# A buffer in front of the weight halves grows by 64 bytes

## The chip, the cores and the metric

The kernel runs on one core of one Trainium2 chip, in one launch. The metric is the device time of the whole program in microseconds (us); lower is better. Most executions of one kernel agree within 0.3%.

## The reference

The input is a sequence of 256 tokens of width 1024, in fp32. It passes through two layers of one kind and one of another, and all matrix products are fp32:

```python
for l in range(2):
    mod = silu(c) @ ada_w[l] + ada_b[l]                     # nine vectors of 1024
    x = x + 0.5 * g1 * swiglu(modulate(rms_norm(x)), w_gate, w_up, w_down)   # d_ff = 2816
    h = modulate(rms_norm(x)); z = h @ w_in[l]
    x = x + g2 * (concat(pool(z), mla_attention(z)) @ w_out[l])
    x = x + 0.5 * g3 * swiglu(modulate(rms_norm(x)), ...)
x = rms_norm(x)
# then one hybrid layer: S5 state-space mixer beside attention, then again
x = x + rmsnorm(swiglu(rmsnorm(x), w_gate, w_up, w_down))   # d_ff = 2816
```

There are five feed-forward networks (FFNs) with `swiglu(h) = (silu(h @ w_gate) * (h @ w_up)) @ w_down`. The S5 mixer needs the powers of a rotation, cos and sin of n times an angle for n up to 255.

## The kernel before

**Products in three passes.** Every weight and every activation of the large products is split into a high part of type fp32r and the rest. Line 539 (`passes`) then makes each product from three matmuls: high by high (L541), high by low (L542), low by high (L543). TensorE reads two operands from SBUF for each: the weights, which a weight load (LDWEIGHTS, "PEld" in the profile) puts into the array, and the moving operand. The profile lists the moving operand first: `gu_bank<-hT_hi,gu_hi` moves hT_hi past the weights gu_hi.

**An FFN.** Its hidden width is cut into 22 blocks of 128. For each block, `gate_up` runs 2 x 8 x 3 = 48 matmuls of 256 columns with weights from gu_hi and gu_lo, and `down` runs 4 x 3 = 12 matmuls of 512 columns with weights from act_hi and act_lo, moving dn_hi and dn_lo. Beside it SyncE loads raw_gu (1 MB) and raw_dn (0.5 MB) for later blocks, ScalarE copies them into gu_hi and dn_hi (L1037, L1043), and VectorE subtracts to get gu_lo and dn_lo (L1374, L1389). ScalarE and VectorE also turn the block's result into act_hi and act_lo (L1049, L1394, L1398, L1400). All of it is double buffered.

**The modulation.** VectorE sums 72 chunks of the matrix ada, 1 MB each, into acc_m and acc_g (L1315, L1325), in spare time beside the FFNs. GpSimd issues most of the loads into `stage`; the first eight come from SyncE into `pro`, `ring` and `stage` at the start of the program.

**The order of the work** is written by hand for each engine, with semaphores between them; no scheduler decides it.

**The buffers.** SBUF addresses follow from the order in which `program` makes the buffers: each starts behind the one before it, at a multiple of 32 bytes, and buffers of one stage share the room of another's. The address of a buffer is the same in all 128 partitions. All that lies behind `wpow` in this order is concerned by the change. Start addresses in bytes (per partition), with the place of each within 128 bytes:

| buffer, or the part that an instruction reads | start | within 128 |
|---|---|---|
| x, xn, hT, hT_hi, hT_lo, raw_gu, raw_dn, dn_hi, dn_lo, ring, gate_b | 16,512 to 118,912 | 0 |
| unit matrix and `fold` in cst | 123,240; 123,752 | 104 |
| ones | 132,576 | 96 |
| cz, its 32-column pieces 128 bytes apart | 133,696 | 64 |
| wpow, 320 bytes | 138,304 | 64 |
| stage, and in its room later ecos | 138,624 | 0 |
| acc_m (later esin), acc_g (later row_b) | 155,008; 175,488 | 0 |
| pro; gu_hi; z; u2 | 183,680 | 0 |
| gu_lo; qn | 200,064 | 0 |
| act_hi, act_lo | 220,544; 222,592 | 0 |
| pieces 0 and 2 of upad, behind their 16 columns of padding | 212,416; 214,592 | 64 |
| the four sums of pooling, behind their padding | from 216,768 | 64 |

All the rows with 0 lie 128 bytes past a multiple of 256.

`wpow` itself (rows 0 and 1: cos and sin of the present power; 2 to 4: scratch) is used while the table of rotations is built:

```python
w_c, w_s = (wpow[:, r, ss_].unsqueeze(2).to_broadcast(wide) for r in (0, 1))   # L1621
step.did(dve.tensor_tensor(wpow[:, 2, :], wpow[:, 0, :], wpow[:, 0, :], ALU.mult))   # L1631
step.then(dve.tensor_tensor(wpow[:, 4, :], wpow[:, 0, :], wpow[:, 1, :], ALU.mult))  # L1633
```

Of the kernel before, what the change touches and what calls it, by code (L numbers as in the profile page):

```python
# [24 lines left out]
P = 128  # L25
# [24 lines left out]
ST = 16  # L50
# [59 lines left out]
def program(nc, x_in, positions, consts, cols, gate_rows, rows, ada, ffn_gu, ffn_dn, mix_w, mix2_w, out):  # L110
    ctx = ExitStack()
    with ctx:
# [6 lines left out]
        def sb(stack, name, shape, dt=F32):  # L119
            return stack.enter_context(nc.sbuf_tensor(name, shape, dt))  # L120
# [30 lines left out]
        cim = sb(ctx, "cim", [P, ST])  # L151
        cz = sb(ctx, "cz", [P, 2, ST, 2, 16])
        sp = sb(ctx, "sp", [P, 8, ST])
        wpow = sb(ctx, "wpow", [P, 5, ST])
        ident = cst[:, C_ID:C_ID + P]
        fold = cst[:, C_FOLD:C_FOLD + P]
        mask = cst[:, C_MASK:C_MASK + 384]
# [1790 lines left out]
```

## Time and profile before

| | |
|---|---|
| median of 3 runs | 1384.41 us (1383.36 to 1385.72) |
| the profiled execution, its own time | 1385.61 us |
| its span, first to last instruction | 1383.8 us |
| mean granted clock of TensorE | 0.967 of full speed |
| TensorE busy | 95% of the span, 8744 matmuls |
| VectorE, ScalarE, GpSimd busy | 76%, 44%, 10% |
| moved by DMA | 296 MB |

The span is one execution seen by the hardware profiler; 1.8 us of that execution's time lie outside it. "Busy" is the union of an engine's instructions. Matmuls overlap in a pipeline, so the mean duration of one (286 ns) is longer than the distance from one start to the next, and what a matmul costs is read from the starts in the timeline.

### The profile page before, as it was taken

Reading aid. Unit: us, or ns where it says so; the run is one execution under the profiler, and the core shown is the slowest. Engines: PE = TensorE matmul, PEld = TensorE weight load, DVE = VectorE, ACT = ScalarE, POOL = GpSimd, SP = SyncE. Lnnn points to the kernel's source line nnn. Section 1 sums busy time; section 2 is a strip of 40 time slices with the busy share of each in tenths; the row PEclk is TensorE's granted clock in tenths of the full one; section 3 lists DMA queues with packets and bytes.
Section 4 is the critical chain, followed back from the end, with each engine's and each line's share of the span. In section 5 each row is a group of like instructions: output and inputs, shape, how many; then the busy total and the mean of one; then the engine's idle time right before and its main releaser. Section 6 shows DMA issues by size and latency. Waiting matters only on the chain.

```text
span 1383.8 us, 21395 instructions
## 1 busy us (share of the span) xinstructions
PE 1308.9 (95%) x8744; PEld 1198.2 (87%) x8744; DVE 1053.2 (76%) x1380; ACT 607.8 (44%) x868; POOL 136.0 (10%) x156
## 2 busy tenths in 40 slices
PE   1999999999999999999999999999978889899998
PEld 1899998989999998999999889999976667899997
DVE  7788887777879548888877868999469996755554
ACT  4533334576333336433345663333362235633333
POOL 0000100000005000100000000000007770000000
PEclk8899999998999999999999989999989989899999
DMA  9699896442886644988974417444442203354541
GB/s 373 254 357 349 339 361 260 144 146 92 305 311 248 261 166 141 361 329 334 352 287 156 160 67 276 182 183 182 184 151 77 76 28 124 144 190 189 189 185 46
DMA packets 55774, 296.12 MB, mean 214 GB/s; under 512 B 6560, under 2 KB 6816, under 8 KB 32416
## 3 DMA queue, kind: packets, MB, share of 16 engines
q1 hardware_dynamic: 46496, 228.21, 45.5%
q0 software_dynamic: 9216, 67.11, 12.2%
q8 instruction: 36, 0.59, 0.2%
q14 instruction: 26, 0.21, 0.0%
HBM read 294.25 MB, written 1.05 MB: 213 GB/s over the span
## 4 chain that ended last, share of the span: by engine, by line
PE 83%; DVE 11%; ACT 3%; issue 2%; DMA 1%; SPq 0%; DVEq 0%; ACTq 0%
PE gu_bank L541 17%; PE gu_bank L543 17%; PE gu_bank L542 17%; PE y_bank L541 8%; PE y_bank L542 8%; PE y_bank L543 8%; DVE ysc L1766 2%; DVE dn_lo L1369 2%; PE t_bank L541 1%; PE t_bank L543 1%; PE t_bank L542 1%; PE t_bank L527 1%; DVE acc_m L1315 1%; DVE vin L1761 1%; DMA pro<-ada 1%
## 5 line engine op out<-in xcount | busy, mean ns | idle before, releaser
L541 PE MATMUL gu_bank<-hT_hi,gu_hi 128*128 128x256 f32 x1760 | 504.2, 286 | 6.5 <-DVE hT_lo L1356 6.5
L542 PE MATMUL gu_bank<-hT_lo,gu_hi 128*128 128x256 f32 x1760 | 502.0, 285 | 0.0
L543 PE MATMUL gu_bank<-hT_hi,gu_lo 128*128 128x256 f32 x1760 | 501.9, 285 | 0.0
L541 PEld LDWEIGHTS gu_bank<-hT_hi,gu_hi 128*128 128x128 f32 x1760 | 341.7, 194 | 12.8 <-issue 9.0
L542 PEld LDWEIGHTS gu_bank<-hT_lo,gu_hi 128*128 128x128 f32 x1760 | 341.9, 194 | 4.7 <-issue 1.0
L543 PEld LDWEIGHTS gu_bank<-hT_hi,gu_lo 128*128 128x128 f32 x1760 | 341.6, 194 | 0.0
L1374 DVE TENSOR_TENSOR gu_lo<-raw_gu,gu_hi 128x2048 fp32r<-128x2048 f32 x105 | 241.1, 2296 | 47.6 <-ACT gu_hi L1037 47.4
L1049 ACT ACTIVATE sg<-gu_bank 128x256 f32<-128x256 f32 x110 | 42.2, 384 | 482.6 <-PE gu_bank L543 482.6
L1037 ACT ACTIVATE gu_hi<-raw_gu 128x2048 fp32r<-128x2048 f32 x105 | 200.6, 1911 | 9.2 <-DMA raw_gu<-ffn_gu 9.2
L541 PE MATMUL y_bank<-dn_hi,act_hi 128*128 128x512 f32 x440 | 172.8, 393 | 0.0
L542 PE MATMUL y_bank<-dn_lo,act_hi 128*128 128x512 f32 x440 | 172.5, 392 | 0.0
L543 PE MATMUL y_bank<-dn_hi,act_lo 128*128 128x512 f32 x440 | 171.2, 389 | 0.0
L1394 DVE TENSOR_TENSOR prod<-sg,gu_bank 128x256 f32<-128x256 f32 x110 | 46.1, 419 | 146.3 <-ACT sg L1049 145.6
L1043 ACT ACTIVATE dn_hi<-raw_dn 128x1024 fp32r<-128x1024 f32 x110 | 116.5, 1059 | 68.2 <-PE y_bank L543 68.2
L1389 DVE TENSOR_TENSOR dn_lo<-raw_dn,dn_hi 128x1024 fp32r<-128x1024 f32 x110 | 134.8, 1226 | 11.0 <-ACT dn_hi L1043 11.0
L468 POOL DMA_DIRECT2D stage<-ada x64 | 36.6, 572 | 793.9 <-DVE acc_g L1325 526.9
L1369 DVE TENSOR_TENSOR dn_lo<-ring,dn_hi 128x1024 fp32r<-128x1024 f32 x70 | 86.5, 1244 | 29.4 <-ACT dn_hi L1015 28.8
L543 PEld LDWEIGHTS y_bank<-dn_hi,act_lo 128*128 128x128 f32 x440 | 82.6, 188 | 18.0
L1015 ACT ACTIVATE dn_hi<-ring 128x1024 fp32r<-128x1024 f32 x70 | 73.5, 1055 | 52.2 <-PE gu_bank L543 23.9
L541 PEld LDWEIGHTS y_bank<-dn_hi,act_hi 128*128 128x128 f32 x440 | 83.0, 189 | 15.4 <-issue 1.0
L1315 DVE SCALAR_TENSOR_TENSOR acc_m<-stage,c_act,acc_m 128x2048 f32<-128x2048 f32 x37 | 87.4, 2363 | 9.7 <-DMA stage<-ada 9.2
L542 PEld LDWEIGHTS y_bank<-dn_lo,act_hi 128*128 128x128 f32 x440 | 83.0, 189 | 13.1
(337 smaller groups left out, 1801.0 us busy)
## 6 DMA issues: line engine op xcount, KB each, us to landing
raw_gu<-ffn_gu SPq DMA_DIRECT2D x110, 1024.0 KB, 5.9
stage<-ada POOLq DMA_DIRECT2D x64, 1024.0 KB, 7.5
raw_dn<-ffn_dn SPq DMA_DIRECT2D x110, 512.0 KB, 3.7
ring<-mix_w SPq DMA_DIRECT2D x72, 512.0 KB, 3.6
pro<-ada SPq DMA_DIRECT2D x5, 1024.0 KB, 12.1
gate_b<-gate_rows SPq DMA_DIRECT2D x6, 512.0 KB, 3.8
stage<-ada SPq DMA_DIRECT2D x2, 1024.0 KB, 20.4
x<-x_in SPq DMA_DIRECT2D x1, 1024.0 KB, 6.1
```

The lines of the kernel that those rows point to most:

```text
L541: pe.matmul(to, a[0], b[0], start=start, stop=False)
L542: pe.matmul(to, a[0], b[1], start=False, stop=False)
L543: return pe.matmul(to, a[1], b[0], start=False, stop=stop)
L1015: act.activation(dn_hi[:, (m + 2) % SLOTS, :], ring[:, n % RING, :], ACT.Copy).then_inc(w_hi_done, 1)
L1037: act.activation(gu_hi[:, b, :, :, :].rearrange("p h c n -> p (h c n)"), raw_gu[:, b, :], ACT.Copy).then_inc(gu_hi_done, 1)
L1043: act.activation(dn_hi[:, b, :], raw_dn[:, b, :], ACT.Copy).then_inc(dn_hi_done, 1)
L1049: act.activation(sg[:, b, :], gu_bank[b][:, 0:S], ACT.Silu).then_inc(silu_done, 1)
L1315: acc.did(dve.scalar_tensor_tensor(to, src, c_act[:, at:at + 1], to, ALU.mult, ALU.add))
L1369: dve.tensor_tensor(dn_lo[:, (m + 2) % SLOTS, :], ring[:, n % RING, :], dn_hi[:, (m + 2) % SLOTS, :].bitcast(F32), ALU.subtract).then_inc( ...
L1374: dve.tensor_tensor(gu_lo[:, b, :, :, :].rearrange("p h c n -> p (h c n)"), raw_gu[:, b, :], gu_hi[:, b, :, :, :].rearrange("p h c n -> p ...
L1389: dve.tensor_tensor(dn_lo[:, b, :], raw_dn[:, b, :], dn_hi[:, b, :].bitcast(F32), ALU.subtract).then_inc(dn_lo_done, 1)
L1394: dve.tensor_tensor(prod[:, b, :], sg[:, b, :], gu_bank[b][:, S:2 * S], ALU.mult).then_inc(prod_done, 1)
```

## The change

`wpow` gets a sixth row of 16 numbers. No instruction reads or writes it. The buffers that are made behind `wpow` start 64 bytes further on. The instructions of every engine, their number, order and shapes stay as they are; only start addresses differ.

```diff
-        wpow = sb(ctx, "wpow", [P, 5, ST])
+        wpow = sb(ctx, "wpow", [P, 6, ST])
```

So stage, acc_m and acc_g (and ecos, esin, row_b), ma and mb, pro, gu_hi, gu_lo, act_hi, act_lo, and all of the mixers' working buffers move from 0 to 64 within 128 bytes, or from 64 to 0. x, xn, hT and its halves, the raw weights, dn_hi, dn_lo, ring, gate_b, cst, ones and cz stay where they are.

## Rows read from the trace of the kernel before

**Rows 1.** The page: busy time, share of the span, instructions; the granted clock in slices.
```profile
PE 1308.9 (95%) x8744; PEld 1198.2 (87%) x8744; DVE 1053.2 (76%) x1380; ACT 607.8 (44%) x868; POOL 136.0 (10%) x156
...
PEclk8899999998999999999999989999989989899999
```

**Rows 2.** The page: the chain of work that ended last, by engine, share of the span.
```profile
PE 83%; DVE 11%; ACT 3%; issue 2%; DMA 1%; SPq 0%; DVEq 0%; ACTq 0%
```

**Rows 3.** The page's groups: line, engine, op, names, shapes, count | busy us, mean ns.
```profile
L541 PE MATMUL gu_bank<-hT_hi,gu_hi 128*128 128x256 f32 x1760 | 504.2, 286 | 6.5 <-DVE hT_lo L1356 6.5
...
L541 PE MATMUL y_bank<-dn_hi,act_hi 128*128 128x512 f32 x440 | 172.8, 393 | 0.0
```

**Rows 4.** Timeline of TensorE inside an FFN: start us, duration us, instruction.
```profile
603.27 0.40 PE L541 MATMUL y_bank<-dn_hi,act_hi 128*128 128x512 f32 x1
603.50 0.40 PE L542 MATMUL y_bank<-dn_lo,act_hi 128*128 128x512 f32 x1
...
606.01 0.28 PE L541 MATMUL gu_bank<-hT_hi,gu_hi 128*128 128x256 f32 x1
606.13 0.28 PE L542 MATMUL gu_bank<-hT_lo,gu_hi 128*128 128x256 f32 x1
```

**Rows 5.** Timeline of TensorE in a mixer, weights from dn_hi.
```profile
250.17 0.28 PE L541 MATMUL t_bank<-hT_hi,dn_hi 128*128 128x256 f32 x1
250.29 0.28 PE L542 MATMUL t_bank<-hT_lo,dn_hi 128*128 128x256 f32 x1
```

**Rows 6.** Timeline of ScalarE and VectorE over one block of that FFN.
```profile
603.47 0.38 ACT L1049 ACTIVATE sg<-gu_bank 128x256 f32<-128x256 f32 x1 [4.63 <-PE gu_bank L543]
...
611.97 0.39 ACT L1049 ACTIVATE sg<-gu_bank 128x256 f32<-128x256 f32 x1 [4.63 <-PE gu_bank L543]
...
606.44 2.29 DVE L1374 TENSOR_TENSOR gu_lo<-raw_gu,gu_hi 128x2048 fp32r<-128x2048 f32 x1
608.64 1.22 DVE L1389 TENSOR_TENSOR dn_lo<-raw_dn,dn_hi 128x1024 fp32r<-128x1024 f32 x1
```

**Rows 7.** Groups of weight loads, whole trace; the weights are the last name.
```profile
L541 PEld LDWEIGHTS gu_bank<-hT_hi,gu_hi 128*128 128x128 f32 x1760 | 341.7, 194 | 12.8 <-issue 9.0
...
L641 PEld LDWEIGHTS y_bank<-sq,ones 128*128 128x128 f32 x20 | 3.5, 191 | 0.3
...
L703 PEld LDWEIGHTS t_bank<-kn,qn 128*128 128x128 f32 x16 | 2.7, 191 | 0.2
...
L671 PEld LDWEIGHTS y_bank<-rot,cst 128*128 128x128 f32 x4 | 0.6, 190 | 0.0
```

**Rows 8.** Groups of plain fp32 matmuls, whole trace; the moving operand is named first.
```profile
L641 PE MATMUL y_bank<-sq,ones 128*128 128x256 f32 x20 | 5.0, 379 | 0.0
...
L703 PE MATMUL gu_bank<-kn,qn 128*128 128x256 f32 x8 | 2.4, 380 | 0.0
...
L684 PE MATMUL gu_bank<-sumA,ring 128*128 128x256 f32 x4 | 1.2, 379 | 0.0
```

**Rows 9.** Groups of ScalarE: copies and squares out of PSUM, 256 columns.
```profile
L1091 ACT ACTIVATE sq<-gu_bank 128x256 f32<-128x256 f32 x6 | 2.2, 365 | 0.0
...
L1073 ACT ACTIVATE upad<-gu_bank 128x256 f32<-128x256 f32 x4 | 1.5, 365 | 0.0
```

**Rows 10.** Groups of VectorE with two inputs in SBUF.
```profile
L1374 DVE TENSOR_TENSOR gu_lo<-raw_gu,gu_hi 128x2048 fp32r<-128x2048 f32 x105 | 241.1, 2296 | 47.6 <-ACT gu_hi L1037 47.4
L1389 DVE TENSOR_TENSOR dn_lo<-raw_dn,dn_hi 128x1024 fp32r<-128x1024 f32 x110 | 134.8, 1226 | 11.0 <-ACT dn_hi L1043 11.0
L1315 DVE SCALAR_TENSOR_TENSOR acc_m<-stage,c_act,acc_m 128x2048 f32<-128x2048 f32 x37 | 87.4, 2363 | 9.7 <-DMA stage<-ada 9.2
...
L1494 DVE TENSOR_TENSOR sumA<-upad 128x1084 f32<-128x1084 f32 x2 | 2.6, 1288 | 3.5 <-ACT upad L1073 3.5
```

**Rows 11.** The page: DMA issues, KB each, median us from issue to landing.
```profile
raw_gu<-ffn_gu SPq DMA_DIRECT2D x110, 1024.0 KB, 5.9
stage<-ada POOLq DMA_DIRECT2D x64, 1024.0 KB, 7.5
```

**Rows 12.** The chain that ended last, in order of time: its first long piece.
```profile
3.59 12.06 DMA pro<-ada
```

**Rows 13.** Timeline of TensorE at the start of a later FFN, and windows with the granted clock (last but two).
```profile
332.24 0.41 PE L543 MATMUL gu_bank<-hT_hi,gu_lo 128*128 128x256 f32 x1
332.45 0.41 PE L541 MATMUL gu_bank<-hT_hi,gu_hi 128*128 128x256 f32 x1
...
332.00:334.00 2.00, 2.00 (x11) 2.00 (x11) 2.00 (x4) 1.88 (x4) 0.00 (x0) 0.50 0.57 238
336.00:338.00 2.00, 2.00 (x18) 2.00 (x18) 1.98 (x1) 1.98 (x2) 0.00 (x0) 0.97 0.00 0
```

## The prediction

> **What bounds the kernel now.** The change moves addresses and nothing else, so the question is which instructions touch a moved address, and whether they are the ones that set the time. I read the busy shares first, then the chain that ended last, then the spacing of matmuls in the timeline. TensorE is busy for 95% of the span [rows 1] and holds 83% of the chain [rows 2]. Most of that is the FFN: three groups of 1760 matmuls on gu_bank and three of 440 on y_bank, of which one each is shown [rows 3]. Inside an FFN the matmuls start 0.12 us apart at 256 columns; the twelve of 512 columns take 606.01 - 603.27 = 2.74 us, 0.228 us each [rows 4]. One block is 48 x 0.120 + 2.74 = 8.50 us, and from one block's sg to the next it is 611.97 - 603.47 = 8.50 us [rows 6]. So nothing but matmuls stands in the block: it is bound by TensorE's own pace, which is the same in every block. ScalarE and VectorE have room: the gu_lo that is made from 606.44 to 608.73 is wanted when the next down (12 matmuls, from about 611.8) is over, near 614.5, some 5.8 us later, and the dn_lo that ends at 609.86 is wanted near 611.8, 1.9 us later [rows 6].
>
> **What the 64 bytes touch on TensorE.** These are the weights of all 5280 gate/up matmuls (gu_hi, gu_lo) and of all 1320 down matmuls (act_hi, act_lo): 6600 of the 8744. The moving operands of the FFN (hT_hi, hT_lo, dn_hi, dn_lo) stay. Before, weights and moving operands all start at 0 within 128 bytes; afterwards the weights start at 64. The spacing has a part that does not scale with columns: 256 columns more cost 0.228 - 0.120 = 0.108 us, so some 12 ns of each matmul are fixed [rows 4]. This is the part a weight load can reach, and the whole effect hangs on it. **Cost taken: 0.** The reasons are rows in which an operand already starts elsewhere. Weight loads of 128 columns take 191 ns from qn (0 within 128), 191 ns from ones (96) and 190 ns from fold in cst (104) [rows 7]; gu_hi's 194 ns is the longest of these four, though it starts at 0, so 64 bytes are not what makes a load long. Matmuls of 256 plain fp32 columns take 380 ns when both operands start at 0 (kn, qn), 379 ns when the weights start at 96 (sq, ones), and 379 ns when the moving operand starts at 64, as the pooling's sums do (sumA, ring) [rows 8]. That last row is the very shift of this change, on the other operand. In the mixers, with weights from dn_hi, the matmuls also start 0.12 us apart [rows 5]; within 512 bytes dn_hi starts at 128 and gu_hi at 384, so at least a shift by 256 bytes does nothing. What no row shows is an fp32r weight load that starts at 64 within 128. Its bounds come from the fixed 12 ns. Upwards: if a load of 512 bytes went in pieces of 128, it would meet five pieces in place of four, 12 / 4 = 3 ns more for each, and 6600 x 3 = 20 us. Downwards: if weights and moving operand hindered each other because they start alike, the 12 ns could go, 6600 x 12 = 79 us less. The nearest rows (rows 7 and 8) differ by 1 ns at most, in both directions and without order, so I take 0 and treat the two ends as rivals.
>
> **ScalarE.** It writes gu_hi, sg and the mixers' buffers at moved places. Two of the four pieces of upad start at 64 and two at 0 within 128; the mean of their writes is 365 ns, as for sq, which starts at 0 [rows 9]. Cost 0. Were each copy 10% longer (0.19 us on 1.9), it would still lie in the 5.8 us before gu_lo is wanted.
>
> **VectorE.** Its subtractions read one or two moved buffers. 1024 columns take 1226 ns and 2048 take 2296 ns, 1.045 ns a column. The pooling's first sum reads upad twice, one element (4 bytes) apart, over 1084 columns: the line gives 1226 + 60 x 1.045 = 1289 ns, measured 1288 ns [rows 10]. Operands that are out of step by 4 bytes cost nothing, so 64 bytes should not. Cost 0, with 1.9 us of cover in a block if that is wrong; outside the FFNs VectorE's 11% of the chain [rows 2], 152 us, has no such cover, and even 1 ns in 400 there would be 0.4 us. The instructions on wpow itself keep their lengths and places within a partition.
>
> **DMA.** Of the loads, those of ada move (64 from GpSimd's queue, seven of the first eight from SyncE's), and a few into row_b and wg; the raw weights stay. The trace has no row that isolates a load by its start within 128 or 256 bytes, so I bound it. Where a load stands in the chain it is once, 12.06 us for the first chunks [rows 12]; the waits of acc_m on stage come to 9.2 us in all [rows 10], inside the cover above. Two kinds of 1 MB load land in 5.9 and 7.5 us [rows 11], 27% apart for reasons of queue and traffic. If the move cost as much, the start would be 12.06 x 0.27 = 3.3 us longer; if it gave as much, 3.3 us shorter. Both kinds start at the same place within 256 bytes, so their difference is no sign of an effect of place, and I take 0, keeping ±3.3 us for the bounds.
>
> **The sum.** TensorE 0, ScalarE 0, VectorE 0, DMA 0. The profiled execution took 1385.61 us, 1383.8 of them in the span; the same is expected of the kernel after it. Against the median of the runs, 1.2 us lower, the forecast is 1384.4 us.
>
> **Rivals.**
> (a) *Slower: the weight load pays for its start.* Each of the 6600 loads becomes longer in the part that is not hidden behind the matmul before it. For it: this is the one thing that no row shows, and TensorE has no slack, so all of it would count. Against it: rows 7 and 8. It decides from 2.8 us / 6600 = 0.42 ns a load. At 1 ns it gives 1384.4 + 6.6 = 1391 us, at 3 ns 1404 us.
> (b) *Faster: the two reads of TensorE get out of each other's way.* The fixed 12 ns shrink by some or all: 1378 us at 1 ns, 1305 us at 12. The other engines would allow it, since a block would be 60 x 12 ns = 0.7 us shorter and the tightest cover is 1.9 us. For it: the fixed part is a delay beyond the columns, since at the lower of the two clocks (granted 0.50, 1.2 GHz) the spacing is 0.21 us, hardly more than the 0.108 us of 256 columns at full clock doubled [rows 13]. Against it: where the starts differ, in fp32, nothing is gained [rows 8], and the fixed part is the same with weights from dn_hi [rows 5].
> (c) *The start of the program moves.* DMA into pro and stage is slower or faster by up to 3.3 us: 1381.1 to 1387.7 us. Only the first 35 us would show it. Most of this lies within what three runs differ by.
> A change that does nothing at all is the forecast itself: I would not be able to tell it from one that costs a tenth of a nanosecond a load.
>
> **How the numbers follow.** No change: 0.84. Rival (a): 0.07. Rival (b): 0.04. Rival (c) in its outer part, beyond 0.2%: 0.05, of which 0.03 slower and 0.02 faster. A measurement of this kernel can tell about 0.2%, 2.8 us, from no change: the three runs differ by 2.4 us. That gives faster 0.06, same 0.84, slower 0.10. The range takes in no change with its spread (1384.4 ± 2.8) and a little of (c) on the upper side: 1381.5 to 1387.8 us, and leaves out some 15 in 100.
>
> **What the profile after would show.** If right: gate/up matmuls 0.12 us apart, down matmuls 0.23, a block of 8.50 us; gu_bank groups at 283 to 286 ns, gate/up weight loads at 194 ns; gu_lo at 2.29 us, gu_hi at 1.91; TensorE's granted clock at 0.967 within a few thousandths, with its dips at the same places, between the FFNs and at the start [rows 1]. If (a) or (b): a spacing other than 0.120 in gate/up while the mixers' matmuls on dn_hi keep theirs. If (c): everything behind the first matmul shifted by a constant, with the first chunks landing at another time. The forecast is wrong above all if the fp32r load reads memory in another way than the plain fp32 one, since my rows for other starts are plain fp32; and it would be wrong without any of this if the clock of TensorE were granted differently, since matmuls at the lower clock are 0.21 us apart in place of 0.12 [rows 13].

## The result

| | before | changed |
|---|---|---|
| median | 1384.4 us | 1359.7 us (1359.1 to 1361.9, four runs) |
| ratio | | 0.983, 95% interval 0.981 to 0.984 |
| span of the profiled execution | 1383.8 us | 1357.3 us |
| TensorE busy | 1308.9 us | 1282.4 us |

The kernel is 24.7 us faster, 1.8%, where no change was forecast. The page of the changed kernel gives busy times, the granted clock and the costliest groups:

```profile
PE 1282.4 (94%) x8744; PEld 1167.1 (86%) x8744; DVE 1050.6 (77%) x1380; ACT 608.8 (45%) x868; POOL 136.3 (10%) x156
...
PEclk8899999999999998999999989999989989999999
...
L541 PE MATMUL gu_bank<-hT_hi,gu_hi 128*128 128x256 f32 x1760 | 494.6, 281 | 8.3 <-DVE hT_lo L1356 8.0
...
L541 PEld LDWEIGHTS gu_bank<-hT_hi,gu_hi 128*128 128x128 f32 x1760 | 334.2, 190 | 15.7 <-issue 9.6
...
L1374 DVE TENSOR_TENSOR gu_lo<-raw_gu,gu_hi 128x2048 fp32r<-128x2048 f32 x105 | 241.0, 2295 | 40.5 <-ACT gu_hi L1037 40.5
...
L541 PE MATMUL y_bank<-dn_hi,act_hi 128*128 128x512 f32 x440 | 173.9, 395 | 0.0
```

TensorE's busy time fell by 26.5 us, just as much as the span; VectorE's subtraction takes 2295 ns as before (2296, [rows 10]) and the granted clock dips in the same stages as before, some dips shorter and some longer [rows 1]. Where TensorE gained is seen in its timeline (start, duration, instruction): the twelve down matmuls from 600.23 to 603.02, then gate/up.

```profile
600.23 0.39 PE L541 MATMUL y_bank<-dn_hi,act_hi 128*128 128x512 f32 x1
600.45 0.40 PE L542 MATMUL y_bank<-dn_lo,act_hi 128*128 128x512 f32 x1
...
603.02 0.28 PE L541 MATMUL gu_bank<-hT_hi,gu_hi 128*128 128x256 f32 x1
603.14 0.28 PE L542 MATMUL gu_bank<-hT_lo,gu_hi 128*128 128x256 f32 x1
...
603.48 0.28 PE L542 MATMUL gu_bank<-hT_lo,gu_hi 128*128 128x256 f32 x1
...
603.93 0.28 PE L543 MATMUL gu_bank<-hT_hi,gu_lo 128*128 128x256 f32 x1
```

From 603.02 to 603.93 are eight steps, 0.114 us each, against 0.120 before [rows 4]. The twelve down matmuls take 2.79 us against 2.74: they became slower. Over all starts in the two traces the mean step from a gate/up matmul to the next instruction fell from 122.0 to 116.3 ns (the slow clock's steps are in both means), 5280 x 5.7 = 30.1 us; from a down matmul it rose from 229.1 to 233.0 ns, 1320 x 3.9 = 5.1 us. The difference, 25.0 us, is 94% of the 26.5. The clock has little part in it: 88 gate/up steps ran at the lower clock before and 67 after, 21 x 0.1 = 2 us, and TensorE's waits at the starts of the second and fifth FFN, some 2 us longer, take that back. The other 1.5 us lie in the steps of the other matmuls (1.7 us less) and ahead of the first one (0.3 us more).

Of these 1.7 us, 0.4 have the cause that the experiments will show. 192 matmuls of the mixers have weights in dn_hi and dn_lo, which stay, and move lat_hi and lat_lo, which the change shifts by 64 bytes. Eight steps of them before and after:

```profile
275.71 0.28 PE L541 MATMUL gu_bank<-lat_hi,dn_hi 128*128 128x256 f32 x1
...
276.67 0.28 PE L543 MATMUL gu_bank<-lat_hi,dn_lo 128*128 128x256 f32 x1
```
```profile
270.92 0.28 PE L541 MATMUL gu_bank<-lat_hi,dn_hi 128*128 128x256 f32 x1
...
271.86 0.28 PE L543 MATMUL gu_bank<-lat_hi,dn_lo 128*128 128x256 f32 x1
```

They take 0.96 and 0.94 us; over the whole trace the step fell from 120.0 to 117.8 ns. The mixers' matmuls that move hT past dn, neither of which moved, stay at 119.8 ns. What is left of the 1.7 us was not traced to a cause.

The timeline of ScalarE in the same FFN: one block is 616.91 - 608.67 = 8.24 us, where it was 8.50 [rows 6].

```profile
608.67 0.39 ACT L1049 ACTIVATE sg<-gu_bank 128x256 f32<-128x256 f32 x1 [4.32 <-PE gu_bank L543]
...
616.91 0.39 ACT L1049 ACTIVATE sg<-gu_bank 128x256 f32<-128x256 f32 x1 [4.32 <-PE gu_bank L543]
```

But in the first half of the second FFN a block takes 356.39 - 347.95 = 8.44 us:

```profile
347.95 0.39 ACT L1049 ACTIVATE sg<-gu_bank 128x256 f32<-128x256 f32 x1 [3.11 <-PE gu_bank L543]
...
356.39 0.38 ACT L1049 ACTIVATE sg<-gu_bank 128x256 f32<-128x256 f32 x1 [4.53 <-PE gu_bank L543]
...
364.84 0.38 ACT L1049 ACTIVATE sg<-gu_bank 128x256 f32<-128x256 f32 x1 [4.53 <-PE gu_bank L543]
```

Of 87 undisturbed blocks in this trace (all 60 steps at the full clock and none with a wait), 78 take 8.24 us and 9 take 8.45; before, all 87 took 8.50. So the same code with the same addresses runs at more than one pace, and that became the second question.

### The profile page after: what moved, and what is told of

The parts are those of the page before. It is cut to its first block, busy times and chain, and to the rows that moved or that the text cites. A ratio compares the mean times of both kernels' runs of the same rounds, so it can differ in the third digit from the quotient of the medians.

```text
span 1357.3 us, 21395 instructions
## 1 busy us (share of the span) xinstructions
PE 1282.4 (94%) x8744; PEld 1167.1 (86%) x8744; DVE 1050.6 (77%) x1380; ACT 608.8 (45%) x868; POOL 136.3 (10%) x156
## 4 chain that ended last, share of the span: by engine, by line
PE 83%; DVE 11%; ACT 3%; issue 1%; DMA 1%; SPq 0%; DVEq 0%; ACTq 0%
PE gu_bank L541 17%; PE gu_bank L542 16%; PE gu_bank L543 16%; PE y_bank L543 8%; PE y_bank L542 8%; PE y_bank L541 8%; DVE ysc L1766 2%; DVE dn_lo L1369 1%; PE t_bank L541 1%; PE t_bank L543 1%; PE t_bank L542 1%; DVE acc_m L1315 1%; DVE xn L1432 1%; DVE vin L1761 1%; DMA pro<-ada 1%
## 5 line engine op out<-in xcount | busy, mean ns | idle before, releaser
L541 PE MATMUL gu_bank<-hT_hi,gu_hi 128*128 128x256 f32 x1760 | 494.6, 281 | 8.3 <-DVE hT_lo L1356 8.0
L543 PE MATMUL gu_bank<-hT_hi,gu_lo 128*128 128x256 f32 x1760 | 491.2, 279 | 0.0
L542 PE MATMUL gu_bank<-hT_lo,gu_hi 128*128 128x256 f32 x1760 | 491.1, 279 | 0.0
L541 PEld LDWEIGHTS gu_bank<-hT_hi,gu_hi 128*128 128x128 f32 x1760 | 334.2, 190 | 15.7 <-issue 9.6
L542 PEld LDWEIGHTS gu_bank<-hT_lo,gu_hi 128*128 128x128 f32 x1760 | 334.8, 190 | 5.4 <-issue 1.0
L543 PEld LDWEIGHTS gu_bank<-hT_hi,gu_lo 128*128 128x128 f32 x1760 | 333.7, 190 | 0.0
L1374 DVE TENSOR_TENSOR gu_lo<-raw_gu,gu_hi 128x2048 fp32r<-128x2048 f32 x105 | 241.0, 2295 | 40.5 <-ACT gu_hi L1037 40.5
L1037 ACT ACTIVATE gu_hi<-raw_gu 128x2048 fp32r<-128x2048 f32 x105 | 201.1, 1915 | 11.9 <-DMA raw_gu<-ffn_gu 11.7
L543 PE MATMUL y_bank<-dn_hi,act_lo 128*128 128x512 f32 x440 | 174.2, 396 | 0.0
L1043 ACT ACTIVATE dn_hi<-raw_dn 128x1024 fp32r<-128x1024 f32 x110 | 116.7, 1061 | 71.6 <-PE y_bank L543 71.5
```

The source lines that it names most:

```text
L541: pe.matmul(to, a[0], b[0], start=start, stop=False)
L542: pe.matmul(to, a[0], b[1], start=False, stop=False)
L543: return pe.matmul(to, a[1], b[0], start=False, stop=stop)
L1037: act.activation(gu_hi[:, b, :, :, :].rearrange("p h c n -> p (h c n)"), raw_gu[:, b, :], ACT.Copy).then_inc(gu_hi_done, 1)
L1043: act.activation(dn_hi[:, b, :], raw_dn[:, b, :], ACT.Copy).then_inc(dn_hi_done, 1)
L1374: dve.tensor_tensor(gu_lo[:, b, :, :, :].rearrange("p h c n -> p (h c n)"), raw_gu[:, b, :], gu_hi[:, b, :, :, :].rearrange("p h c n -> p ...
```

## The experiments

**Which buffer: only gu, only act, or everything.** Three kernels, each the kernel before with gaps put between buffers.

Only gu_hi and gu_lo move by 64 bytes:

```diff
+        sb(work, "gu_gap", [P, 16])
         gu_hi = sb(work, "gu_hi", [P, 2, 2, KC, P], F32R)
         ...
+        sb(work, "act_gap", [P, 112])
         act_hi = sb(work, "act_hi", [P, 2, S], F32R)
```

> Only gu_hi and gu_lo (with sg and prod, which lie behind them) move by 64 bytes; act_hi and act_lo move by 512 bytes and so keep their place within 512, and everything else stays where the kernel before has it. Theory A (the weights' start sets the pace of TensorE, each buffer for itself): gate/up matmuls at about 0.114 us, down matmuls back at 0.227 to 0.229, time about 1384.4 - 30 = 1354 us, 5 us below the changed kernel. Rival B (the gain comes from another moved buffer: stage, pro, acc_m or the mixers' buffers): 1384 us, spacing 0.120. Rival C (what matters is the distance between gu and act, which is unchanged in the changed kernel and here becomes 448 bytes more): something else, above 1360 us.

Measured: 1372.4 us, ratio 0.990 (0.989 to 0.992). It is faster, so gu counts, but it gave less than half of what was expected (12.4 of 30 us). Its blocks take 615.34 - 606.94 = 8.40 us:

```profile
606.94 0.39 ACT L1051 ACTIVATE sg<-gu_bank 128x256 f32<-128x256 f32 x1 [4.53 <-PE gu_bank L545]
...
615.34 0.38 ACT L1051 ACTIVATE sg<-gu_bank 128x256 f32<-128x256 f32 x1 [4.53 <-PE gu_bank L545]
```

The down matmuls are back at 229.2 ns (mean of all starts), as theory A says, but the gate/up matmuls stand at 117.8 ns in every undisturbed block, not at 113.4.

Only act_hi and act_lo move by 64 bytes:

```diff
+        sb(work, "act_gap", [P, 16])
         act_hi = sb(work, "act_hi", [P, 2, S], F32R)
```

> Only act_hi and act_lo move by 64 bytes, all else stays as in the kernel before. Theory A: gate/up at 0.120 us, down matmuls alternate between 0.231 and 0.236, time about 1384.4 + 5 = 1389.5 us. Rival B and C: 1384 us.

Measured: 1387.6 us, ratio 1.0025 (1.0015 to 1.0034), down matmuls at 233.8 ns, gate/up at 119.5 (119.8 before) and a block of 8.54 us. The slower down matmuls alone cost what was expected, within 2 us. Together the two kernels save 12.4 and lose 2.8 us, 9.6 us, where the changed kernel saves 24.7: the effects don't add.

Everything moves by 64 bytes:

```diff
+        sb(ctx, "first_gap", [P, 16])
         x = sb(ctx, "x", [P, TT, D])
```

> All buffers of the kernel before move by 64 bytes, x and hT and the raw weights too, so that all distances between buffers stay as before. Theory A1 (the place of the weights relative to the moving operand counts): no change, 1384 us, 0.120 us for gate/up. Theory A2 (the weights' own place counts, wherever the moving operand starts): 0.114 us for gate/up and 0.2335 for down, about 1359 us. If the mixers' matmuls (weights dn_hi, moving hT_hi) stay at 0.120 it is A1; if they too go to 0.114, A2.

Measured: 1385.4 us, ratio 1.000 (0.999 to 1.001). Gate/up is at 0.120 again, and a block at 612.10 - 603.60 = 8.50 us:

```profile
603.60 0.38 ACT L1050 ACTIVATE sg<-gu_bank 128x256 f32<-128x256 f32 x1 [4.63 <-PE gu_bank L544]
...
612.10 0.38 ACT L1050 ACTIVATE sg<-gu_bank 128x256 f32<-128x256 f32 x1 [4.63 <-PE gu_bank L544]
```

Here stage, pro and the mixers' buffers lie where the changed kernel has them, and gu and act too. The moving operands hT and dn moved with them, and the gain is gone. So it is the distance between weights and moving operand that counts, not the weights' own place (theory A1), and the loads into stage and pro are not the cause. The distance between gu and act is the changed kernel's too, so rival C falls with it.

**The effect by itself.** A kernel with nothing but streams of 48 matmuls:

```python
for r in range(48):
    c, h = r % 4, r % (1024 // cols)
    pe.matmul(bank[(r // 8) % 2][:, 0:cols], wt[:, P * c:P * (c + 1)], mv[:, cols * h:cols * (h + 1)], start=True, stop=True)
```

> Not the computation: a stream of 48 fp32r matmuls for each pair of a weight buffer and a moving buffer, nothing else running beside TensorE. Weights of 128 columns start at 0, 32, ... 480 within 512 bytes, the moving operand of 256 or 512 columns at 0; then weights at 0 and 64 with the moving operand at 32, 64, 128 and 256. Theory A: with weights at 0 a group of 48 lasts 48 x 0.120 = 5.8 us, at 64 48 x 0.114 = 5.5 us (256 columns), and 10.9 against 11.2 us for 512 columns; the moving operand at 64 with weights at 64 gives 0.120 again under A1 and 0.114 under A2. If the effect needs ScalarE, VectorE or DMA at work beside it (rival D, contention with other engines), all groups of one width last equally long.

Measured, from the groups of this kernel (busy us of a whole stream of 48, then the mean ns of one; `mv64x,wt0x` is the moving operand at 64 and the weights at 0 within 512 bytes):

```profile
L63 PE MATMUL bk<-mv64x,wt64x 128*128 128x256 f32 x48 | 5.9, 283 | 0.0
L63 PE MATMUL bk<-mv0x,wt0x 128*128 128x256 f32 x48 | 5.9, 283 | 0.0
...
L63 PE MATMUL bk<-mv0x,wt256x 128*128 128x256 f32 x48 | 5.9, 283 | 0.0
...
L63 PE MATMUL bk<-mv0x,wt64x 128*128 128x256 f32 x48 | 5.8, 281 | 0.0
...
L63 PE MATMUL bk<-mv64x,wt0x 128*128 128x256 f32 x48 | 5.6, 276 | 0.0
```

and as mean steps between starts in ns, without each stream's first eight (moving operand at 0, weights at the place in the head; 256 to 480 gave the same as 0 to 224 within 0.2 ns):

| | 0 | 32 | 64 | 96 | 128 | 160 | 192 | 224 |
|---|---|---|---|---|---|---|---|---|
| 256 columns | 120.0 | 118.4 | 117.8 | 117.4 | 118.7 | 119.9 | 117.8 | 117.8 |
| 512 columns | 226.8 | 233.4 | 233.4 | 234.4 | 232.6 | 233.3 | 228.9 | 233.3 |

With both operands at 64 the steps are 120.0 and 226.7, as with both at 0. So TensorE alone does it, without VectorE, ScalarE or DMA beside it (rival D falls); the pace goes with the distance within 256 bytes; and the place that is worst for 256 columns (0) is the best for 512. The 0.114 us expected at 64 did not come: it is 117.8 ns here. Two pairs did not fit at 256 columns. Weights at 0 with the moving operand at 64 is a distance of 192, and ran at 113.3 ns where two other pairs with that distance (192 and 0, 64 and 128) ran at 117.8. Weights at 0 with the moving operand at 32 is a distance of 224, and ran at 116.7 ns where the table has 117.8. The first is taken up below; the second stayed open.

**The FFN's buffers alone.** gu and act both by 64, and nothing outside the FFN:

```diff
+        sb(work, "gu_gap", [P, 16])
         gu_hi = sb(work, "gu_hi", [P, 2, 2, KC, P], F32R)
```

> The FFN's buffers alone (gu_hi, gu_lo, sg, prod, act_hi, act_lo) move by 64 bytes; stage, pro, acc_m, acc_g, row_b and all of the mixers' buffers stay where the kernel before has them. Moving gu alone gave 1372 us (0.118 us a gate/up matmul, not 0.114), moving act alone 1387.5, the sum of both effects would be 1375, and the changed kernel has 1359.7. Theory E (the pace of the gate/up matmuls depends on the state in which the down matmuls before them leave TensorE, so gu and act have to be moved together): 0.1135 us for gate/up, about 1360 us. Rival B (the missing 12 us come from stage, pro or the mixers' buffers): about 1372 to 1375 us and 0.118 us.

Measured: 1358.5 us (four executions, 1357.7 to 1359.7), ratio 0.981 (0.980 to 0.983), the whole gain. A fifth, the one that was profiled, took 3298 us, with most gate/up steps at 0.25 us or more; the reason isn't known, and so no trace shows the expected 0.1135 us for this kernel. Rival B falls by the time: what stage, pro, acc_m and the mixers' buffers give (0.3 us in the matmuls that read lat_hi and lat_lo, by the traces above) is less than the times can tell.

**Pairs of places.** The FFN's rhythm of 48 gate/up and 12 down matmuls on TensorE alone:

```python
for gp in PH:              # gu's place, 0 to 224
    for ap in PH:          # act's place
        for n in range(3):
            gate_up(gp, n % 2)
            down(ap)
```

> Not the computation: blocks of 48 gate/up matmuls (256 columns) and 12 down matmuls (512 columns) in three passes, as in an FFN, on TensorE alone, three blocks for each pair of a place of the gate/up weights and a place of the down weights within 256 bytes (0 to 224 in steps of 32 each), the moving operands at 0. Theory E: the second and third block last 8.50 us with both at 0, 8.25 with both at 64, about 8.40 with gu at 64 and act at 0, 8.55 with gu at 0 and act at 64; other pairs may be faster than the changed kernel's. Rival D' (the interplay comes from ScalarE, VectorE or semaphores in the FFN): gate/up at 0.118 with gu at 64 whatever act's place, so 8.40 to 8.46 us.

Measured, us a block, mean of the second and third (a quarter of the table; rows: gate/up weights, columns: down weights):

| | 0 | 64 | 128 | 192 |
|---|---|---|---|---|
| 0 | 8.50 | 8.54 | 8.53 | 8.50 |
| 64 | 8.40 | 8.24 | 8.35 | 8.20 |
| 128 | 8.53 | 8.49 | 8.47 | 8.49 |
| 192 | 8.38 | 8.45 | 8.45 | 8.41 |

The four blocks of the four full kernels come out to a hundredth: 8.50 (before), 8.24 (changed), 8.40 (gu only), 8.54 (act only). Rival D' falls, since act's place changes gate/up's pace with no other engine at work, and theory E stands. The best of all 64 pairs is 64, 192 and the worst 160, 96 (8.57). For the pair 64, 0 the first block, entered from another pair, still ran at 113.5 ns, and the second and third at 117.8, with the same operands. Starts of the first and of the second block:

```profile
429.79 0.28 PE L62 MATMUL bk<-hThi,g64hi 128*128 128x256 f32 x1
...
430.92 0.28 PE L63 MATMUL bk<-hTlo,g64hi 128*128 128x256 f32 x1
```
```profile
437.78 0.28 PE L62 MATMUL bk<-hThi,g64hi 128*128 128x256 f32 x1
...
438.96 0.28 PE L63 MATMUL bk<-hTlo,g64hi 128*128 128x256 f32 x1
```

Ten steps each: 1.13 and 1.18 us.

**Other number types.** The same streams with bf16 and with plain fp32 operands:

> Not the computation: streams of 32 matmuls with bf16 operands and then with plain fp32 operands, 256 and 512 columns, weights at 0 to 224 within 256 bytes in steps of 32, the moving operand at 0. Plain fp32: if the rows of the kernel before tell the whole of it, 0.216 us at 256 columns wherever the weights start. bf16: if the effect belongs to fp32r, 0.107 to 0.11 us at 256 columns at every place; if it belongs to the fast way of loading weights, the spacing differs between places by some ns.

Measured: no difference between any two of the eight places of the weights; the moving operand stayed at 0.

```profile
L65 PE MATMUL bk<-mfx,wf0x 128*128 128x256 f32 x64 | 14.0, 379 | 0.0
L65 PE MATMUL bk<-mfx,wf64x 128*128 128x256 f32 x64 | 14.0, 379 | 0.0
...
L65 PE MATMUL bk<-mbx,wb0x 128*128 128x256 bf16 x32 | 3.7, 273 | 0.0
L65 PE MATMUL bk<-mbx,wb64x 128*128 128x256 bf16 x32 | 3.7, 272 | 0.0
```

The steps are 215.8 ns (plain fp32, two records to a matmul) and 109.2 ns (bf16) at 256 columns, 429.2 and 215.8 at 512. These types have next to no part that does not scale with columns, whatever the place: bf16 takes 215.8 - 109.2 = 106.6 ns for 256 more columns and 109.2 for the first 256. In fp32r, columns over the full clock (106.7 and 213.3 ns) leave 7 to 13 ns at 256 columns and 13 to 21 at 512, and only this part moves.

**Is there a better pair?** gu by 64 and act by 192:

```diff
+        sb(work, "gu_gap", [P, 16])
         gu_hi = sb(work, "gu_hi", [P, 2, 2, KC, P], F32R)
         ...
+        sb(work, "act_gap", [P, 32])
         act_hi = sb(work, "act_hi", [P, 2, S], F32R)
```

> gu_hi, gu_lo, sg and prod 64 bytes further on than in the kernel before, act_hi and act_lo 192 bytes, all else as before. Theory E, with the pace read from the stream of block pairs on TensorE alone: gate/up 0.1136 us, down 0.229, a block of 8.20 us in place of 8.50, so 1384.5 - 110 x 0.30 = 1351.5 us, some 8 us under the changed kernel. If the changed kernel's 8.25 is the best that this does in company of the other engines: 1359 us.

Measured: 1358.8 us, ratio 0.980 (0.979 to 0.982), not told apart from the changed kernel, and its runs spread from 1355.9 to 1364.1. Its profile (that of the 1364.1) has 53 blocks of 8.20 us and 34 of 8.46: the first two FFNs run at 117.9 ns throughout, the other three at 113.6. In the slower blocks the down matmuls are slower too, 233.5 ns against 229.0. The 34 blocks of 87 are some 43 of all 110, and 43 x 0.26 = 11 us: without them this execution would have come to some 1353 us, near the 1351.5 that were expected.

The same distances, made by moving hT's halves instead of gu:

```diff
+        sb(ctx, "hT_gap", [P, 48])
         hT_hi = sb(ctx, "hT_hi", [P, KC, S], F32R)
         ...
+        sb(ctx, "raw_gap", [P, 16])
         raw_gu = sb(ctx, "raw_gu", [P, 2, 2 * KC * P])
         ...
+        sb(work, "act_gap", [P, 48])
         act_hi = sb(work, "act_hi", [P, 2, S], F32R)
```

> The same two distances for the FFN (weights of gate/up 64 bytes past the moving operand's place within 256, of down 192), but made by moving the other side: hT_hi and hT_lo start 64 bytes back within 256 relative to gu, which keeps its place relative to all else; act_hi and act_lo 192 further. By that the mixers' 768 matmuls with weights from dn_hi and moving hT_hi get the distance of 64 too. Theory A1 (only the distance within 256 counts): the FFNs as in the kernel with 64 and 192, 8.20 us a block, and the mixers' matmuls at 0.113 to 0.118 in place of 0.120, 1.5 to 5 us more: 1347 to 1350 us. If the weights' own place counted after all: 0.120 in gate/up and about 1384 us.

Measured: 1359.7 us, ratio 0.981 (0.980 to 0.983). gu keeps its place relative to all else and the gain is there, so A1 holds from this side too. The expected 1347 to 1350 was missed for the most part by slower blocks again: 55 blocks of 8.21 us and 32 of 8.42. Taken to all 110 blocks that is 40 x 0.21 = 8 us, without which it would be some 1351 us; the rest of the miss was not traced. In the mixers the matmuls on dn_hi, now at a distance of 64 too, run at 113 to 118 ns where it had been 120.

High and low half of gu at separate places, down weights at 192:

> Not the computation: the stream of block pairs on TensorE alone with the down weights at 192, and the high and the low half of the gate/up weights at separate places (0 to 224 within 256, steps of 32, all 64 pairs). Theory: pairs with both at 64 give 8.20 us a block and both at 0 8.50; where the halves differ, a matmul's pace lies between those of its own two places, so no pair is much below 8.20 unless the order of the places matters, then down to 8.1.

Measured, in us a block: 8.50 with both at 0, 8.20 with both at 64; high at 192 and low at 64, and both at 192, give 8.19 (8.41 for both at 192 in the table above; the next experiment shows why that can be), and no pair less, so separate places for the halves open nothing below 8.2. Six of the 64 pairs ran above 8.50, the slowest (160, 128) at 8.74: differing halves are not always between their own two places.

**Two rhythms.** What picks 113.4 or 117.8 ns, the operands or the moment?

```python
for gp, ap in ((64, 64), (64, 192), (64, 0), (192, 192)):
    for k in range(1, 17):
        pe.matmul(bank[0][:, 0:16 * k], src[:, 0:P], src[:, 0:16 * k], start=True, stop=True)   # plain fp32
        for n in range(3):
            gate_up(gp, n % 2)
            down(ap)
```

> Not the computation: blocks of 48 gate/up and 12 down matmuls on TensorE alone, for four pairs of places (gate/up, down): 64,64; 64,192; 64,0; 192,192. Before every three blocks stands one plain fp32 matmul of 16, 32, ... 256 columns, so that the stream starts at 16 different moments. Theory F (at a distance of 64 there are two settled rhythms, 0.1134 and 0.1178 us, and the moment at which the stream starts picks one): the third block lasts 8.2 us after some starts and 8.4 to 8.45 after others, with the same operands; 64,64 would be fast after most (78 of 87 plain blocks in the changed kernel), 64,192 after some 6 in 10, 64,0 after none, 192,192 after some. Rival G (the rhythm hangs on the operands alone, and the slow halves in the kernels come from other engines): the third block of a pair lasts the same after every start.

Measured, gate/up of the third block after 16 different starts:

| gu, act | in the fast rhythm | in the slow rhythm (117.8 ns) |
|---|---|---|
| 64, 64 | 12 (113.4 ns) | 4 |
| 64, 192 | 12 (113.6 ns) | 4 |
| 64, 0 | 0 | 16 |
| 192, 192 | 2 (113.3 ns) | 14 |

The third block of 192, 192 after 32 columns and after 48 columns, ten steps each, 1.13 and 1.18 us:

```profile
1266.38 0.28 PE L64 MATMUL bk<-hThi,g192hi 128*128 128x256 f32 x1
...
1267.51 0.28 PE L65 MATMUL bk<-hTlo,g192hi 128*128 128x256 f32 x1
```
```profile
1291.74 0.28 PE L65 MATMUL bk<-hTlo,g192hi 128*128 128x256 f32 x1
...
1292.92 0.28 PE L66 MATMUL bk<-hThi,g192lo 128*128 128x256 f32 x1
```

Theory F stands and rival G falls: with the same operands there are two settled rhythms, and a difference of 16 columns in one matmul ahead of the stream picks one. This also fits the stream above with a distance of 192 that ran at 113.3 ns. And it says why the effects did not add: with act at 0, gu at 64 never settles in the fast rhythm, in sixteen starts out of sixteen.

**The changed kernel once more.**

> The changed kernel once more. Theory F: the median within 2 us of 1359.7, and plain FFN blocks of 8.24 and 8.45 us; the FFN half that settles at 0.1178 may be another one than in the first profile (there it was the first half of the second FFN), or none: 1357.5 us. Rival G (the operands alone decide): the same half in the same rhythm.

Measured: 1359.6 us, ratio 0.982 (0.981 to 0.983). In this profile all 87 undisturbed blocks take 8.24 us, and the span is 1355.4 instead of 1357.3 us. The half that had been slow:

```profile
346.21 0.39 ACT L1049 ACTIVATE sg<-gu_bank 128x256 f32<-128x256 f32 x1 [1.98 <-PE gu_bank L543]
...
354.45 0.39 ACT L1049 ACTIVATE sg<-gu_bank 128x256 f32<-128x256 f32 x1 [4.32 <-PE gu_bank L543]
...
362.69 0.39 ACT L1049 ACTIVATE sg<-gu_bank 128x256 f32<-128x256 f32 x1 [4.32 <-PE gu_bank L543]
```

Nine blocks of 0.21 us are 1.9 us, as much as the two spans differ; that it comes out so closely is in part luck, since other steps differ by up to 1 us both ways. The rhythm of a half is thus a part of what runs of one kernel differ by.

## Why the prediction was wrong

**What bounds the kernel**: right. The block is TensorE's own pace, 48 steps and 12 steps, and 94% of the result lies in these steps. The cover of the other engines was as said: inside the blocks nothing else became late when one shrank by 0.26 us. Outside them a little did: TensorE's wait for hT_lo at the starts of the FFNs grew from 6.5 us in all [rows 3] to 8.0.

**"Cost taken: 0" for TensorE**: the step that failed. It was put that all hangs on the fixed part of each matmul, 12 ns, and that is where the 30.1 us came from. But it was then set to zero by rows that could not speak on it. Rows 8 are plain fp32, and durations instead of steps; in that type 256 columns more cost 429.2 - 215.8 = 213.4 ns and the first 256 cost 215.8, so only 2.4 ns are fixed, and the step is the same at every place of the weights. Rows 7 are durations of weight loads, most of which lie under a matmul; gu_hi's went from 194 to 190 ns while the step went from 120 to 113.4. Rows 5, an fp32r stream from other buffers, differ from rows 4 by 256 bytes, which is exactly one period. In fact every fp32r product in the kernel before had its operands at a distance of 0 within 256 bytes, the slowest of the eight for 256 columns, so its trace showed a single point of a curve and looked like a constant. Put as a term of the sum: TensorE stood there with 0 and measured -25.0 us, -30.1 in gate/up and +5.1 in down. The prediction named the fp32r load as its weakest point, and still gave rivals (a) and (b) only 0.11 together.

**Rival (b)**, faster because the two reads of TensorE get out of each other's way, with 0.04: the right side, and its place, the fixed part, is right. Its size was off, as was one sign: it gave 1 to 12 ns on all 6600 matmuls; measured were 5.7 ns less on 5280 and 3.9 ns more on 1320. That the reads collide in SBUF is still only an argument; what the runs show is the dependence on the distance.

**Rival (a)**, a weight load that pays for its start: in gate/up the other way round. The down matmuls did become slower, by 3.9 ns, close to the 3 ns of its upper end by luck, not because their start is odd: with the moving operand shifted along, the streams of 512 columns are back at 226.7 ns.

**ScalarE, VectorE**: right, 1915 and 2295 ns for the large operations (1911 and 2296 before). **DMA**: right as far as the time goes; the first chunks land after 12.34 us (12.06 before, [rows 12]) and stage after 7.8 (7.5, [rows 11]), and the kernel in which these loads kept their places had the same time as the changed one. Neither number follows the place: where everything moved the first chunks, moved alike, landed after 11.93 us, and stage also took 7.8 us in the kernels that moved only gu or only act. The 0.1 us that the prediction estimated from the Trainium skill (DMA: Bandwidth & Descriptors, How a descriptor splits into AXI transactions) is below what any run here can show.

**The clock**: right, 0.971 against 0.967, and worth 2 us at most, as counted above.

## What to carry to other kernels

Where TensorE is the bound, measure the step from one matmul's start to the next, compare it with columns over clock, and ask of what remains whether it depends on where the operands lie; for fp32r, try the weights 64 bytes further on within 256 than the moving operand, and try each width of matmul at a place of its own (in streams on TensorE alone that gave 8.20 us a block instead of 8.24; in the full kernel the runs could not tell it apart). Evidence on a cost must come from instructions of the same type that have that cost at all; rows in which all places are alike modulo the period are one observation, not many. A gain of this kind is a settled rhythm that small disturbances can switch, so take several runs and count blocks before calling one placement better than another.

## What the hardware showed that was not expected

- fp32r matmuls of 256 columns step at 113.3 to 120.0 ns and of 512 columns at 226.7 to 234.4 ns, depending on where the operands lie and on the rhythm they settled in; the period is 256 bytes of distance. bf16 and plain fp32 don't care about the place of the weights.
- The best distance for one width is not the best for another: in the plain streams 0 is the slowest of the eight at 256 columns (120.0 ns) and the fastest at 512 (226.8).
- Two rhythms, 113.4 and 117.8 ns, exist for the same operands. At the lower clock, 1.2 GHz, the fixed part is not to be seen, 0.21 us a step [rows 13]; what holds the stream up at the higher one was not found.
